# Final norm of a decoder step in three batches of token tiles, two of the five tiles multiplied on GpSimd and ScalarE

## What is computed

```python
def rmsnorm(x, g):
    xf = x.astype(jnp.float32)
    xf = xf * lax.rsqrt(jnp.mean(xf * xf, axis=-1, keepdims=True) + EPS)
    return xf.astype(x.dtype) * g
...
    return rmsnorm(x, norm_final), ...
```

## Time and profile before

| what | value |
|---|---|
| median of three runs | 1349.48 us (1349.31 to 1349.58) |
| the profiled execution's own time | 1349.23 us |
| its span in the profile | 1347.4 us |
| mean granted clock of TensorE | 0.971 |
| busy: TensorE, VectorE, ScalarE, GpSimd | 93%, 62%, 45%, 11% |
| first load of the final norm issued | 1328.77 us |
| last pass of VectorE begins | 1343.11 us |
| last store issued | 1344.42 us |

### The profile page before, as it was taken

The page is one execution under the profiler, slowest core; times in us unless marked ns, Lnnn a source line. Parts: engine busy times, 40 slices in busy tenths (PEclk is TensorE's granted clock), DMA queues, the critical chain, the costliest instruction groups (busy, mean ns, idle before and its releaser), DMA issues.

```text
span 1347.4 us, 18886 instructions
## 1 busy us (share of the span) xinstructions
PE 1248.3 (93%) x6184; PEld 807.3 (60%) x6185; DVE 831.6 (62%) x1352; ACT 608.9 (45%) x826; POOL 145.8 (11%) x158
## 2 busy tenths in 40 slices
PE   7999999899999999999999999799999999999992
PEld 5888854477574747464656576264747474656550
DVE  3896668699393837464655596182937464655643
ACT  4111342478273545354444574172735354453632
POOL 8100011010001010101101000100010101101000
PEclk9999999989999999999999999999999999999996
DMA  9610176399999999999999984999999999999984
GB/s 322 87 38 1 52 259 287 131 334 411 355 417 412 419 411 419 405 422 405 414 409 400 416 364 180 406 419 406 421 408 421 404 412 397 401 417 388 421 341 139
DMA packets 67333, 457.16 MB, mean 339 GB/s; under 512 B 15916, under 2 KB 19508, under 8 KB 34520
## 3 DMA queue, kind: packets, MB, share of 16 engines
q1 hardware_dynamic: 56344, 435.28, 78.9%
q0 software_dynamic: 10944, 21.30, 6.7%
HBM read 440.26 MB, written 23.50 MB: 344 GB/s over the span
## 4 chain that ended last, share of the span: by engine, by line
PE 42%; DMA 20%; DVE 8%; issue 5%; ACT 4%; DVEq 0%; SPq 0%; ACTq 0%; POOLq 0%; POOL 0%
PE bank L2144 24%; DMA ring_lo<-in_w_gate_up 15%; PE bank L2254 12%; DVE w_lo L2376 6%; DMA ymix<-ffn_in,idx_next 3%; ACT w_hi L1964 3%; PE bank L2265 2%; DMA token_sums<-ymix,row_cur 1%; PE bank L2134 1%; PE bank L2127 1%; DVE cmix L2394 1%; DVE cmix L2397 1%; PE bank L2230 1%; ACT cmix L1983 0%; PE bank L2274 0%
## 5 line engine op out<-in xcount | busy, mean ns | idle before, releaser
L2376 DVE TENSOR_TENSOR w_lo<-ring_lo,w_hi 128x1024 fp32r<-128x1024 f32 x271 | 315.6, 1220 | 101.0 <-ACT w_hi L1964 99.9
L1964 ACT ACTIVATE w_hi<-ring_lo 128x1024 fp32r<-128x1024 f32 x271 | 270.2, 1052 | 86.8 <-DMA ring_lo<-in_w_gate_up 64.4
L2254 PE MATMUL bank<-ring_lo,x_s 128*64 128x512 f32 x960 | 215.9, 597 | 0.4 <-ACT x_s L1973 0.4
L2144 PE MATMUL bank<-w_hi,x_hi 128*128 128x512 f32 x544 | 179.5, 412 | 8.9 <-DVE x_lo L2382 6.7
L2144 PE MATMUL bank<-w_lo,x_hi 128*128 128x512 f32 x544 | 173.8, 402 | 0.0
L2144 PE MATMUL bank<-w_hi,x_lo 128*128 128x512 f32 x544 | 172.2, 398 | 0.0
L2376 DVE TENSOR_TENSOR w_lo<-w_out,w_hi 128x1024 fp32r<-128x1024 f32 x136 | 161.7, 1220 | 6.0 <-ACT w_hi L1964 5.2
L1964 ACT ACTIVATE w_hi<-w_out 128x1024 fp32r<-128x1024 f32 x136 | 140.0, 1053 | 31.8 <-PE bank L2144 31.6
L1892 POOL DMA_INDIRECT token_sums<-ymix,row_cur x33 | 57.2, 1732 | 742.3 <-ACT ymix L1994 705.3
L2254 PEld LDWEIGHTS bank<-ring_lo,x_s 128*64 128x64 f32 x960 | 65.0, 137 | 119.1 <-issue 117.0
L2144 PEld LDWEIGHTS bank<-w_hi,x_hi 128*128 128x128 f32 x544 | 102.4, 196 | 40.1 <-issue 18.8
(11 more groups left out here) (444 smaller groups left out, 1407.4 us busy)
## 6 DMA issues: line engine op xcount, KB each, us to landing
ring_lo<-in_w_gate_up SPq DMA_DIRECT2D x128, 2048.0 KB, 18.8
w_out<-in_w_down SPq DMA_DIRECT2D x128, 1024.0 KB, 20.5
ring_lo<-in_w_in SPq DMA_DIRECT2D x3, 2048.0 KB, 21.1
w_out<-in_w_out SPq DMA_DIRECT2D x2, 2048.0 KB, 8.7
x<-in_x_prompt SPq DMA_DIRECT2D x6, 512.0 KB, 11.3
bias<-bias_rows SPq DMA_DIRECT2D x132, 3.0 KB
ring_lo<-in_w_in SPq DMA_DIRECT2D x2, 1024.0 KB, 9.7
token_sums<-x SPq DMA_DIRECT2D x4, 512.0 KB
```

The lines of the kernel that those rows point to most:

```text
L1964: nc.scalar.activation(high(j), raw(j), ACT.Copy).then_inc(s["w_hi"], 1)
L2144: last = nc.tensor.matmul(bank[b + u][:], v[:, k, :], part(j)[:, u, :], start=(j == 16 and first), stop=(k == KD - 1 and part is high and ...
L2254: last = nc.tensor.matmul(bank[2 * half][64 * u:64 * u + 64, :], x_s[:, k % 4, 64 * (k // 4):64 * (k // 4) + 64], gu[:, k, :, half, 256 * ...
L2376: v.tensor_tensor(low(j), raw(j), high(j).bitcast(F32), ALU.subtract).then_inc(s["w_lo"], 1)
```

## The change

The final norm's bookkeeping is grouped. Positions are taken in three batches, (0), (1, 2) and (3, 4): `variance`, `root` and `inverse` are issued once for a batch, on one or two columns. The tiles of positions 0 and 1 are no longer multiplied by VectorE: GpSimd multiplies each with the weight vector into the free buffer `weighted`, and ScalarE, behind all its squares and roots, multiplies by the row's value into `total(q)` and raises a new semaphore `fin_act`. VectorE keeps `output` for positions 2, 3 and 4. SyncE stores in the same order of positions as before, 0 and 1 on `fin_act`, the others on `fin`. The semaphores `weighted` and `fin_act` are two that the mixer has done with.

```diff
@@ -216,7 +216,8 @@
     keep["spent"] = {"g_in": (wglu_in, 16), "sq": (s["gel_sig"], MT), "var": (s["gel_in"], MT), "root": (s["glu_psum"], MT),
                      "fin": (s["y_gelu"], MT), "stored": (s["out_done"], 7 * 16), "step": (s["crow"], 1), "sums": (s["crow_psum"], 1),
                      "bias_in": (s["u_blk_in"], 16 * (CH + 1)), "acc_set": (s["u_stored"], 16), "bdn_in": (s["toep"], 16 * CH),
-                     "x_s": (s["p_ready"], 1), "s_first": (s["arow"], 1), "s_used": (s["par"], 1), "row": (s["exps"], 1)}
+                     "x_s": (s["p_ready"], 1), "s_first": (s["arow"], 1), "s_used": (s["par"], 1), "row": (s["exps"], 1),
+                     "weighted": (s["k_psum"], 2), "fin_act": (s["k_sb"], 2)}
 
     def taken(eng, n):
 
@@ -1764,11 +1765,19 @@
     ssf = keep["pcol"][:, 0:3 * NT].rearrange("p (a i) -> p a i", a=3)
     junk = keep["ring_lo"][:, 0:2, :]
     gfin = keep["x"][:, 0, :]
+    weighted = keep["ring_lo"][:, 2:4, :]
     TILES = keep["tiles"]
+    BY_ACT = 2
+    BATCHES = ((0,), (1, 2), (3, 4))
     outs = 1 + (NT - 2) + 2
     x_in = keep["x_in"]
     t = {n: v[0] for n, v in keep["spent"].items()}
     t0 = {n: v[1] for n, v in keep["spent"].items()}
+
+    def batch(c):
+
+        i = [TILES[q] for q in BATCHES[c]]
+        return max(rows(k) for k in i), slice(i[0], i[-1] + 1)
 
     def total(q):
         i = TILES[q]
@@ -1861,8 +1870,12 @@
         for q, i in enumerate(TILES):
             sp.dma_start(total(q), scratch["acc"][i * P:i * P + rows(i)]).then_inc(x_in[i], 16)
         y_p = out["y_p"][0]
-        for q, i in enumerate(TILES):
-            sp.wait_ge(t["fin"], t0["fin"] + q + 1)
+        for q in (0, 1, 2, 3, 4):
+            i = TILES[q]
+            if q < BY_ACT:
+                sp.wait_ge(t["fin_act"], t0["fin_act"] + q + 1)
+            else:
+                sp.wait_ge(t["fin"], t0["fin"] + q - BY_ACT + 1)
             if i == 0:
                 sp.dma_start(y_p[0:P - NMETA, :], total(q)[NMETA:P]).then_inc(t["stored"], 16)
             elif i < NT - 1:
@@ -1950,6 +1963,11 @@
         added(FINAL)
         overflow(pool, over, more)
         pool.sem_inc(t["sums"], 1)
+        pool.wait_ge(t["g_in"], t0["g_in"] + 16)
+        for q in range(BY_ACT):
+            i, n = TILES[q], rows(TILES[q])
+            pool.wait_ge(x_in[i], 48 if i in (0, NT - 1) else 32)
+            nc.gpsimd.tensor_tensor(weighted[0:n, q], total(q), gfin[0:n, :], ALU.mult).then_inc(t["weighted"], 1)
 
     @block.scalar
     def _(act):
@@ -2101,15 +2119,27 @@
             nc.scalar.activation(junk[0:n, q % 2], total(q), ACT.Square, accum_out=ssf[0:n, 2, i:i + 1]).then_inc(t["sq"], 1)
 
         nc.scalar.preload_act_table(ACT.Sqrt)
+        def root(c):
+            n, i = batch(c)
+            act.wait_ge(t["var"], t0["var"] + c + 1)
+            nc.scalar.activation(ssf[0:n, 0, i], ssf[0:n, 2, i], ACT.Sqrt).then_inc(t["root"], 1)
+
+        def scale(q):
+            i, n = TILES[q], rows(TILES[q])
+            act.wait_ge(t["step"], t0["step"] + 5 * q + 5)
+            act.wait_ge(t["weighted"], t0["weighted"] + q + 1)
+            nc.scalar.activation(total(q), weighted[0:n, q], ACT.Copy, scale=ssf[0:n, 0, i:i + 1]).then_inc(t["fin_act"], 1)
+
         square(0)
-        for q, i in enumerate(TILES):
-            n = rows(i)
-            if 1 <= q < NT - 1:
-                square(q + 1)
-            act.wait_ge(t["var"], t0["var"] + q + 1)
-            nc.scalar.activation(ssf[0:n, 0, i:i + 1], ssf[0:n, 2, i:i + 1], ACT.Sqrt).then_inc(t["root"], 1)
-            if q == 0:
-                square(1)
+        square(1)
+        root(0)
+        square(2)
+        square(3)
+        root(1)
+        square(4)
+        root(2)
+        for q in range(BY_ACT):
+            scale(q)
 
     @block.tensor
     def _(pe):
@@ -2513,17 +2543,17 @@
             ins.then_inc(t["step"], 1)
             dve.wait_ge(t["step"], t0["step"] + count[0])
 
-        def variance(q):
-
-            i, n = TILES[q], rows(TILES[q])
-            dve.wait_ge(t["sq"], t0["sq"] + q + 1)
-            v.tensor_scalar(ssf[0:n, 2, i:i + 1], ssf[0:n, 2, i:i + 1], 1.0 / D, EPS, ALU.mult, ALU.add).then_inc(t["var"], 1)
-
-        def inverse(q):
-
-            i, n = TILES[q], rows(TILES[q])
-            dve.wait_ge(t["root"], t0["root"] + q + 1)
-            done(refine_rsqrt(nc, done, ssf[0:n, 0, i:i + 1], ssf[0:n, 1, i:i + 1], ssf[0:n, 2, i:i + 1]))
+        def variance(c):
+
+            n, i = batch(c)
+            dve.wait_ge(t["sq"], t0["sq"] + BATCHES[c][-1] + 1)
+            v.tensor_scalar(ssf[0:n, 2, i], ssf[0:n, 2, i], 1.0 / D, EPS, ALU.mult, ALU.add).then_inc(t["var"], 1)
+
+        def inverse(c):
+
+            n, i = batch(c)
+            dve.wait_ge(t["root"], t0["root"] + c + 1)
+            done(refine_rsqrt(nc, done, ssf[0:n, 0, i], ssf[0:n, 1, i], ssf[0:n, 2, i]))
 
         def output(q):
             i, n = TILES[q], rows(TILES[q])
@@ -2532,13 +2562,14 @@
 
         dve.wait_ge(t["g_in"], t0["g_in"] + 16)
         variance(0)
-        for q in range(NT):
-            if 1 <= q < NT - 1:
-                variance(q + 1)
-            inverse(q)
-            output(q)
-            if q == 0:
-                variance(1)
+        inverse(0)
+        variance(1)
+        inverse(1)
+        output(2)
+        variance(2)
+        inverse(2)
+        output(3)
+        output(4)
 
 
 # ---- launch: one core; inputs and outputs as the reference has them ----
```

## The result

The changed kernel took 1350.72 us (median of 22 runs), the kernel before 1348.99 us beside it (22 runs); ratio 1.0014, 95% interval 1.0008 to 1.0020. By the ratio it is 1.9 us slower, with an interval of 1.1 to 2.7 us: far less than 2%, and of the size that was forecast. Single runs of one kernel scatter by 3 to 4 us.

The account below looks back on a forecast made before the run. VectorE was taken to set the kernel's end; the change gives 0.94 us there but the queue of stores takes 2.84, so +1.9 on 1349.23 makes 1351.1 us, range 1349.6 to 1352.5.

Parts of the forecast that it names:

- the queue of stores: SyncE's queue at the end: four stores issued within 1.3 us, more than the DMA engines can move at once, costing 2.84 us.
- VectorE's gain: Final norm on VectorE: its last pass ends at 1343.45 instead of 1344.39, 0.94 us earlier.
- Landings are not altered: Loads of the final norm: they land as before, so square 3 starts at 1335.94.
- The total, +1.9: Whole span: 1349.3 against 1347.4, from VectorE's 0.94 us gained and 2.84 us taken by the queue of stores.
- rival A's mild form: End of kernel: ScalarE's copies earlier than placed or a cheaper variance, -0.5 to +1.2 us; chance of A 0.13.
- ScalarE's copies: Scaled copies of positions 0 and 1 behind root 2: first begins at 1339.9, they end at 1341.03 and 1342.15.
- Rival A: End of kernel: the backlog of stores is smaller and VectorE's gain shows, 0.94 us earlier if stores were hidden; chance 0.13.
- Rival B: GpSimd and VectorE slow each other's passes: slower by more than 2.7 us, +3.2 with a doubled output 2; chance 0.04.
- 1.4 us of slack: VectorE's small instructions of inverse 0, which GpSimd's passes meet, have 1.4 us to spare before root 1.
- Rival C: Stores at the end: a queue runs slower than single stores, all at 287 GB/s, giving +3.5 us; chance 0.06.

Follow-up runs that it names:

- e11: The changed kernel measured again, unaltered, against the kernel before: ratio 1.0007 (0.9998 to 1.0016).
- e1: The changed kernel with SyncE's stores in the order of positions 2, 0, 1, 3, 4: ratio 0.9999 to the kernel before.
- e2: The kernel before with all stores held until VectorE's last pass is done: ratio 1.0046 to the kernel before.
- e5: The changed kernel with variance 2 ahead of output 2 on VectorE: ratio 1.0005 to the kernel before.
- e6: The changed kernel with e5's order on VectorE and e1's order of stores together: ratio 1.0000 to the kernel before.
- e4: The changed kernel with two more unused passes on GpSimd after its own two: a single run, 1353.39 us.
- e9: The changed kernel without its batches, positions 0 and 1 still over GpSimd and ScalarE: ratio 1.0018 to the kernel before.

## Why the prediction was right

**The deciding term, the queue of stores, held.** Forecast: from the end of the last pass (1343.45) to the end of the span (1349.3) 5.85 us; measured 5.83 and, in e11, 5.85. The parts also: 448 KB at 262 to 287 GB/s and three times 512 KB near 410, full from 1342.5 to 1347.9, which is 5.4 us as forecast. The four stores were issued within 1.7 us and not 1.3, since the issues themselves took 0.32 to 1.26 us; the backlog hid it, as forecast. e1 shows that order alone moves the end, e2 that bunching alone costs time.

**VectorE's gain was under-sized in the profile, by the landing.** Forecast 0.94 us, measured 1.63 (1.49 in e11). "Landings are not altered" was the step: nothing altered them, but they vary. The fourth square started at 6.56 us and 6.76 in the two profiles of the changed kernel, at 7.17 before, at 7.16 and 8.11 in e1 and e5, which are the same up to there. 0.57 of the surplus of 0.69 us is the earlier root 1 that comes of it, and the rest is in the main that a pass is followed 1.20 us after its start (two take 2.48), where I had put 1.28. Whether the change makes late landings rarer stays open.

**The total, +1.9, was met by the first set of runs, and that is partly luck.** The tails of the two profiles give +1.2 and +1.35 us, and the second set of runs +0.9. This is the size of rival A's mild form, copies earlier than I placed them. What the forecast did not say is that the landing now counts in full: before, VectorE asked for root 2 at 1337.77 and had it since 1337.2, 0.6 us early, while the changed kernel's tail moves with the fourth square. An estimate: over the five profiles with its order of squares (the changed kernel, e11, e1, e5, e6) that square starts at 7.19 us in the mean; with 13.24 from there the tail is 20.4, +1.8 against the one profile of before.

**GpSimd**: 2.34 us for a pass, forecast 2.30 from twice; done at 1335.95, forecast 1335.6.

**ScalarE's copies**: 1.13 us each as in the earlier trace rows, 1.04 apart; they ended 0.8 us earlier than forecast against the first load, most of it the landing again.

**Rival A** fell in its main form: there is no gap in the stores, and VectorE's gain did not show. **Rival B** had a real mechanism but a wrong form: I had both engines slower from 3.6 us a pass on. In fact a pass of 2.3 us already holds VectorE to its end, and what counts is which instruction meets it. Here it met inverse 0, for which I had counted 1.4 us of slack. The hold took 1.26 us (line 77), and with the early landing that was all of it: root 1 started 1.10 us after the fourth square, where 1.06 is the least. The forecast had counted on this slack, but against a slower engine, not a stopped one. e4 and e9 show the price without that slack. The Trainium skill (GPSIMD Engine Reference, Key points) names instructions with two SBUF inputs or in a 2-port performance mode as those that contend. e4 agrees for two inputs (1.39 and 2.02 us), and shows that contention means waiting for the whole pass; whether the two-column TENSOR_SCALAR ran in such a mode no view here shows. **Rival C** fell: six slices in a row are at 410 GB/s or more (1344.5 to 1347.5). This stands above the limit of about 358 GB/s for one core that the Trainium skill (DMA: Bandwidth & Descriptors, Specifications) gives. The page's section Measured calls that the share of each core when both cores of a pair stream; here one core ran, so by the page too the limit did not tell against the forecast.

## What to carry to other kernels

At the end of a kernel, count bytes and not only instructions: note when the last store is issued and how much is still unsent then. Taking work off the engine that ends last gains nothing if it lets finished tiles wait, in an in-order queue, behind tiles that a slower path finishes later; store in the order of readiness, and start the big stores early. A helper on GpSimd can stop VectorE for a whole pass, so place it where VectorE has slack. And when small steps are grouped, look at what the grouped one now stands behind: here root 1 came to wait for a load that it does not need.

## What the runs showed of the hardware that was not expected

- A VectorE instruction with two tensors in SBUF, or over two columns of one, waited for the end of the GpSimd pass that ran beside it: 0.15 us became 1.39, 1.41, 2.02, 2.28 and, over two passes, 2.94 us. The same holds in e1, e5, e6 and e11 (1.21, 1.77, 1.65, 1.20 us, each to the end of GpSimd's second pass). One-column single-input instructions did not wait.
- Issuing a store takes longer when others are queued: 0.43, 0.84 and 1.26 us for the three of the changed kernel, 0.45 to 1.22 in e2, against 0.32 to 0.35 with an empty queue. The DMA engines were full meanwhile, so no cost of it is seen here.
- Small stores of 64 and 32 KB held the DMA engines 0.7 to 1.05 busy at 123 to 148 GB/s; in e2 the 96 KB took about 0.75 us, where 512 KB alone took 1.28.
- The store of 112 rows ran at 229 to 295 GB/s in all kernels but e2 and e6, where its stretches show up to 352 GB/s; the stores of 128 rows ran at 377 to 434. Why was not tried.
- The square that waits for the fourth load (or stands right behind the third) started up to 1.5 us apart in five profiles with loads issued alike (6.56 to 8.11 us).
- In e2 and e6 one or two of the 16 DMA engines ended 0.4 to 0.7 us after the others, and the span with them. Why is open.
